# Index weights and index key in one unit of a two-block float32 transformer kernel, and VectorE's small jobs placed anew

## The reference

```python
cond = jax.nn.silu(c)
mod = (cond @ ada_w[l] + ada_b[l]).reshape(B, 6, D_MODEL)[:, :, None, :]
shift1, scale1, gate1 = mod[:, 0], mod[:, 1], mod[:, 2]
shift2, scale2, gate2 = mod[:, 3], mod[:, 4], mod[:, 5]
u = rmsnorm(x, norm_mix[l]) * (1.0 + scale1) + shift1
aq, ak, av, bq, bkv, biq, bik, biw, cq, ck, cv, g = split_cols(u @ w_in[l])
# index branch: 8 heads of 32, key bik (32 columns), head weights biw (8 columns)
s_idx = jax.nn.relu(jnp.einsum('bqhd,bkd->bqhk', iqb, ik))
score = jnp.einsum('bqhk,bqh->bqk', s_idx, iwb).astype(jnp.float32) * idx_scale
_, sel = lax.top_k(score, topk)          # topk = 64
# ... attention over the selected keys, two other attentions, gates, w_o
x = x + gate1 * (merged @ w_o[l])
u2 = rmsnorm(x, norm_mlp[l]) * (1.0 + scale2) + shift2
h = jnp.square(jax.nn.relu(u2 @ w_ff1[l]))
x = x + gate2 * (h @ w_ff2[l])
```

## Time and profile before

| | us |
|---|---|
| runs | 946.45, 946.54, 956.6; median 946.54 |
| profiled execution: its own time | 953.5 |
| its span, first to last instruction | 951.7 |
| TensorE busy in it | 923.2 (97%) |
| VectorE, ScalarE, GpSimd busy | 600.0, 498.3, 694.0 |
| mean granted TensorE clock | 0.985 of 2.4 GHz |

### The profile page before, as it was taken

How to read it: one execution, slowest core, us unless ns; L and a number is a source line. 1 busy time by engine, 2 the same in 40 slices (tenths; PEclk the granted TensorE clock), 3 DMA queues, 4 the chain that set the end, 5 groups by cost and what they waited for, 6 DMA issues and landing times.

```text
span 951.7 us, 21722 instructions
## 1 busy us (share of the span) xinstructions
PE 923.2 (97%) x7684; PEld 903.9 (95%) x7684; DVE 600.0 (63%) x1122; ACT 498.3 (52%) x820; POOL 694.0 (73%) x898
## 2 busy tenths in 40 slices
PE   5899999999999999999999999999999999999996
PEld 5898999989999999999999999999899999999996
DVE  3888878888785443532666677773346666877522
ACT  3555665574567664454644464444535444544451
POOL 1795669778778778877676679888827666788873
PEclk9999999999999999999999999999969999999999
DMA  9995448775545556555354546555514444455521
GB/s 359 415 359 192 165 178 292 289 260 183 178 158 198 205 187 249 194 204 177 136 178 174 176 136 219 177 184 198 194 45 170 149 168 150 160 211 187 201 87 45
DMA packets 28225, 185.22 MB, mean 195 GB/s; under 512 B 3027, under 2 KB 5504, under 8 KB 6272
## 3 DMA queue, kind: packets, MB, share of 16 engines
q1 hardware_dynamic: 25832, 167.93, 48.8%
q10 hardware_dynamic: 2328, 16.40, 4.7%
HBM read 183.26 MB, written 1.07 MB: 194 GB/s over the span
## 4 chain that ended last, share of the span: by engine, by line
PE 88%; DVE 6%; issue 2%; ACT 2%; DMA 1%; SPq 0%; POOL 0%; POOLq 0%; ACTq 0%; DVEq 0%
PE mm L609 26%; PE mm L611 25%; PE mm L610 25%; PE mm L643 1%; DVE score L1683 1%; PE mm L627 1%; PE mm L628 1%; PE mm L629 1%; ACT w_hi L1109 1%; PE ps_s L974 1%; PE ps_o L991 1%; PE ps_o L1065 1%; DMA hot<-onehot 1%; DVE ada_raw L1563 1%; DVE w_lo L1525 1%
## 5 line engine op out<-in xcount | busy, mean ns | idle before, releaser
L526 POOL TENSOR_TENSOR w_lo<-raw,w_hi 128x256 fp32r<-128x256 f32 x880 | 683.7, 814 | 235.2 <-ACT w_hi L1109 235.2
L609 PE MATMUL mm<-u_hi,w_hi 128*128 128x256 f32 x1568 | 447.8, 286 | 0.7 <-issue 0.6
L610 PE MATMUL mm<-u_lo,w_hi 128*128 128x256 f32 x1568 | 436.3, 278 | 0.0
L611 PE MATMUL mm<-u_hi,w_lo 128*128 128x256 f32 x1568 | 436.2, 278 | 0.0
L1109 ACT ACTIVATE w_hi<-raw 128x1024 fp32r<-128x1024 f32 x291 | 307.6, 1058 | 154.8 <-PE mm L611 148.5
L609 PEld LDWEIGHTS mm<-u_hi,w_hi 128*128 128x128 f32 x1568 | 296.4, 189 | 6.0 <-issue 5.3
L610 PEld LDWEIGHTS mm<-u_lo,w_hi 128*128 128x128 f32 x1568 | 296.4, 189 | 2.0 <-issue 1.9
L611 PEld LDWEIGHTS mm<-u_hi,w_lo 128*128 128x128 f32 x1568 | 296.6, 189 | 0.0
L1525 DVE TENSOR_TENSOR w_lo<-raw,w_hi 128x1024 fp32r<-128x1024 f32 x71 | 96.6, 1360 | 64.3 <-ACT w_hi L1109 55.2
L609 PE MATMUL mm<-h_hi,w_hi 128*128 128x256 f32 x256 | 70.8, 277 | 0.0
L610 PE MATMUL mm<-h_lo,w_hi 128*128 128x256 f32 x256 | 70.7, 276 | 0.0
(11 more groups left out here) (350 smaller groups left out, 1339.2 us busy)
## 6 DMA issues: line engine op xcount, KB each, us to landing
raw<-weights SPq DMA_DIRECT2D x145, 1024.0 KB, 4.8
ada_raw<-ada ACTq DMA_DIRECT2D x14, 1024.0 KB, 5.3
ada_raw<-ada SPq DMA_DIRECT2D x6, 1024.0 KB, 9.3
ada_more<-ada SPq DMA_DIRECT2D x4, 1024.0 KB, 12.1
bias<-tab_scratch SPq DMA_DIRECT2D x1, 1536.0 KB, 10.8
dec<-decay ACTq DMA_DIRECT2D x1, 1536.0 KB, 7.1
x<-xT SPq DMA_DIRECT2D x1, 1024.0 KB, 10.7
out<-x SPq DMA_DIRECT2D x4, 256.0 KB, 2.3
```

The lines of the kernel that those rows point to most:

```text
L526: ins = nc.gpsimd.tensor_tensor(lo[:, at], r[:, at], hi[:, at], ALU.subtract)
L609: nc.tensor.matmul(dst, wh, rhs_hi(k), start=a, stop=False)
L610: nc.tensor.matmul(dst, wh, rhs_lo(k), start=False, stop=False)
L611: i = nc.tensor.matmul(dst, wl, rhs_hi(k), start=False, stop=b)
```

## The change

One unit is taken out of the stream: the index key is now held three times in rows 0 to 95 of unit 0 and the 8 index weights in its rows 96 to 103. ACT takes the unit out of PSUM in three instructions (rows 0 to 95 of `ikT`, rows 96 to 127 of `ikT` from rows 0 to 31, and `iwf`). Everything behind unit 2 moves up by one number (290 units). So the tables of the attention are shifted by one, and the units whose `low` is VectorE's stand one place later in every stage. Besides, the index steps are regrouped, the selection rounds are placed anew, `ADA_AT` keeps 24 of 32 sums, and 8 sums (gate2, tiles 20 to 23) go behind eight units of the first MLP matrix, the last two tiles being loaded there from ACT's queue.

```diff
-N_QKV = 27
+N_QKV = 26
-C_IW, C_IQ, C_IK, C_KV, C_BQ = 0, 1, 3, 4, 5
-C_A = 9
-C_C = 21
+C_IW, C_IK, C_IQ, C_KV, C_BQ = 0, 0, 1, 3, 4
+C_A = 8
+C_C = 20
+IW_AT = 96
-    s_at = {12 + 3 * r: r for r in range(12)}
+    s_at = {11 + 3 * r: r for r in range(12)}
-    ADA_AT = [1, 2, 4, 7, 8, 10] + sorted([*range(16, 49, 3)] + [*range(26, 49, 3)] + [*range(30, 49, 3)])
-    LOAD_AT = {ADA_AT[2 * (n - 10) + 1] + 1: n for n in range(10, 24)}
-    IDX_AT = {6: [0], 7: [1], 8: [2, 3], 9: [4], 10: [5, 6], 11: [7]}
+    ADA_AT = [1, 2, 4] + sorted([*range(15, 48, 3)] + [*range(25, 48, 3)] + [44, 47])
+    LOAD_AT = {ADA_AT[2 * (n - 10) + 1] + 1: n for n in range(10, 22)}
+    ADA_F1 = {8: 0, 9: 1, 10: 2, 11: 3, 14: 4, 15: 5, 16: 6, 17: 7}
+    LOAD_F1 = {11: 22, 13: 23}
+    IDX_AT = {6: [0, 1], 7: [2], 8: [3, 4], 9: [5], 10: [6, 7]}
-    TOPK_AT = {10: [0] * 3, 11: [0] * 2, 12: [0], 13: [0] * 2, 16: [1] * 2, 18: [1] * 2, 19: [1], 21: [1] * 2, 22: [1]}
+    TOPK_AT = {10: [0] * 3, 11: [0], 12: [0] * 4, 14: [1], 15: [1] * 2, 17: [1], 18: [1] * 2, 20: [1], 21: [1]}
-    INV_AT = {27: 0, 33: 1, 36: 2, 39: 3}
-    ROOT_AT, FIN_AT, OAH_AT, OAL_AT = 41, 42, 44, 46
+    INV_AT = {26: 0, 32: 1, 35: 2, 38: 3}
+    ROOT_AT, FIN_AT, OAH_AT, OAL_AT = 40, 41, 43, 45
@@ qkv_evac, ScalarE
             if c == C_IW:
-                take_reversed(c, iwf[:, :], 8)
-            elif c < C_IK:
+                bank = bank_of(c)
+                A(ikT[0:IW_AT, :], bank[0:IW_AT, 0:T], ACT.Copy)
+                A(ikT[IW_AT:P, :], bank[0:P - IW_AT, 0:T], ACT.Copy)
+                A(iwf[:, :].rearrange("p (t q) -> p t q", t=QT),
+                  bank[IW_AT:IW_AT + 8, 0:T].rearrange("p (t q) -> p t q", t=QT)[:, :, ::-1], ACT.Copy)\
+                    .then_inc(taken[c % 4], 1)
+            elif c < C_KV:
                 take_reversed(c, iqT[:, c - C_IQ, :])
-            elif c == C_IK:
-                take(c, ikT[:, :])
@@ up_turn, ScalarE
+                if f in LOAD_F1:
+                    ada_load(act, LOAD_F1[f])
@@ VectorE, start of the first MLP matrix
                 low(None, U_F1 + SLOTS)
+                low(None, U_F1 + SLOTS + 1)
-        low(None, U_F1 + 2 * SLOTS)
+        for c in range(U_F1 + SLOTS + 2, U_F1 + 2 * SLOTS + 1):
+            low(None, c)
@@ up_turn, VectorE
+                if f in ADA_F1:
+                    ada_step(5 * KC + ADA_F1[f])
```

More of the change, by code:

```diff
@@ L390, in _build @@
     o_at = {c + 4: r for c, r in s_at.items()}
-    SUB_AT = {18 + 3 * h: h for h in range(NH)}
-    UV_AT = {29 + 3 * h: h for h in range(NH)}
-    VT_AT = {13 + 3 * h: 1 + h for h in range(NH)} | {25: 5, 28: 6}
-    ADA_AT = [1, 2, 4, 7, 8, 10] + sorted([*range(16, 49, 3)] + [*range(26, 49, 3)] + [*range(30, 49, 3)])
-    LOAD_AT = {ADA_AT[2 * (n - 10) + 1] + 1: n for n in range(10, 24)}
-    assert len(ADA_AT) == 4 * KC
-    IDX_AT = {6: [0], 7: [1], 8: [2, 3], 9: [4], 10: [5, 6], 11: [7]}
+    SUB_AT = {17 + 3 * h: h for h in range(NH)}
+    UV_AT = {28 + 3 * h: h for h in range(NH)}
+    VT_AT = {12 + 3 * h: 1 + h for h in range(NH)} | {24: 5, 27: 6}
+    ADA_AT = [1, 2, 4] + sorted([*range(15, 48, 3)] + [*range(25, 48, 3)] + [44, 47])
+    LOAD_AT = {ADA_AT[2 * (n - 10) + 1] + 1: n for n in range(10, 22)}
+    assert len(ADA_AT) == 3 * KC
+    ADA_F1 = {8: 0, 9: 1, 10: 2, 11: 3, 14: 4, 15: 5, 16: 6, 17: 7}
+    LOAD_F1 = {11: 22, 13: 23}
+    IDX_AT = {6: [0, 1], 7: [2], 8: [3, 4], 9: [5], 10: [6, 7]}
     HIGH_AT = {3: 8, 5: 9, 6: 10, 7: 11}
@@ L1818, in _ @@
                     .then_inc(S["oal_ready"], 1)
-        ada_read(dve, 6 * KC - 1)
+        ada_read(dve, 5 * KC - 1)
         o = O_BR
@@ L1949, in _ @@
         low(None, U_F2 - 1 + SLOTS)
+        ada_read(dve, 6 * KC - 1)
         V.tensor_tensor(nf_pre[:, :], vec[:, COLS["norm_final"]:COLS["norm_final"] + KC],
@@ L2241, in _stream @@
     aq, ak, av, bq, bkv, biq, bik, biw, cq, ck, cv, gate = [w_in[:, a:b] for a, b in zip(at[:-1], at[1:])]
-    parts = [_units(np.pad(biw, ((0, 0), (0, P - 8)))), _units(biq), _units(np.concatenate([bik] * 4, axis=1)),
+    parts = [_units(np.concatenate([bik] * 3 + [np.pad(biw, ((0, 0), (0, P - IW_AT - 8)))], axis=1)), _units(biq),
              _units(bkv), _units(bq)]
```

## The result

| | before | after |
|---|---|---|
| median, us | 946.61 | 954.24 |
| lowest to highest of 14 runs | 944.31 to 956.60 | 949.29 to 961.36 |
| profiled execution, span | 953.5, 951.7 | 961.36, 959.6 |

The ratio is 1.0072, 95% interval 1.0044 to 1.0100: the changed kernel is slower by 0.4 to 1.0%. Forecast were 944.0 us and a range of 938.0 to 951.0.

What follows compares the result with a forecast made beforehand. The prediction took TensorE's work plus the places where it stands still as the bound. Its terms summed to -2.5 us, taking the 946.5 median to 944.0, with an 8-in-10 range of 938.0 to 951.0.

Steps and rivals of the forecast that it cites:

- First MLP matrix: First MLP matrix: the wait for GpSimd's `w_lo` of the twelfth unit goes, -0.6 us; the eight sums there cost 0.
- One unit less: TensorE: 24 matmuls go with the removed unit, -2.9 us.
- rival 3: Until unit 22: VectorE sets the pace and its waits eat the removed unit's gain; 946.6 us, chance 0.2.
- Unit 0's way out of PSUM: Before unit 6: ScalarE does five copies instead of three before its bank may be written, +0.2 us.
- First: First `normalise`, transpose of head 0: TensorE waits 2.4 us instead of 1.8, +0.6.
- second normalise: Transpose of head 1: `low` and two rounds in block 15 make TensorE wait 2.1 us instead of 0.4, +1.7.
- Third normalise: Transpose of head 2: the low now stands behind `normalise`, so the 0.92 us wait ends, -0.9.
- Layers: Both layers: the first `low` now stands between q and k, so `kr` comes 0.35 and 0.55 us late, +0.9.
- last heads: Heads 9 and 10: the low now stands behind head 10's `normalise`, -0.8 us; head 9 counted 0.
- branches: Branch units: `low` goes one unit on, ending waits of 0.5 us at the second and 0.25 at the fifth, -0.75.
- 1 (the waits end): Heads 0 and 1: the waits for `normalise` go, and with the first the clock's fall; 938.3 us, chance 0.2.
- rival 2: Unit 17, behind the second `normalise`: the clock falls to half for long, costing 1.6 to 8.3 us; 952.3, chance 0.15.

Runs made afterwards that it cites:

- m1: Kernel before with only the unit merged; index steps, selection rounds and all 32 sums one block earlier: 946.72 us, ratio 1.0011.
- m2: Changed kernel with each of the eight sums in the first MLP matrix replaced by a copy of one column: 948.41 us, ratio 1.0020.
- b2: Changed kernel with the two selection rounds of block 15 put into block 14, nothing else: 951.55 us, ratio 1.0030.
- b3: Changed kernel with only the first half's selection rounds moved, from block 9 on: 955.59 us, ratio 1.0074.
- e7: Changed kernel with MLP sums three units apart, both halves' selection rounds moved, and a low in the layers put behind k's rotation: 942.05 us, ratio 0.9955.
- m3: Changed kernel with the condition row of the eight MLP sums copied once by VectorE to PSUM and read there: 950.96 us, ratio 1.0072.
- e8: Changed kernel with index steps and rounds of the kernel before, one block earlier, and the eight MLP sums three units apart: 945.05 us, ratio 0.9976.
- b1: Changed kernel with e7's selection rounds and the condition row of the dense MLP sums read from PSUM, copied by ScalarE: 941.54 us, ratio 0.9917.
- b4: Kernel before (291 units, nothing merged) with everything else of b1, its tables one block later: 947.39 us, ratio 0.9983.
- c1: b1 with ScalarE's row copy in halves behind units 8 and 9, and sums behind units 10 to 13 and 16 to 19: 941.06 us, ratio 0.9950.

## Why the prediction was wrong

**The step that failed** is *First MLP matrix*: "so it is behind by under 2 us with three banks free before TensorE minds: **0**". It asked who waits for VectorE and never which engine VectorE holds up while it works. The page had GpSimd busy for 694 us, and the trace of before showed the price in the same stage, by tile (least/median/longest ns of a quarter; the longest lie beside VectorE's lows):

```profile
L526 POOL TENSOR_TENSOR w_lo<-raw,w_hi x98: 720/742/1827, 267.2 to 358.1; 128x256 fp32r<-128x256 f32 x98
```

GpSimd has 1.9 us to spare in four units (four of 2.72, less twelve quarters of 0.75), of which a low takes up to 1.0; four sums in four units take 3.8 more. At the stop itself two sums and one low had run: three quarters at 1.7 instead of 0.74, 2.9 us more in a stretch of 5.8. Without the sums (m1, m2) TensorE waits 0.5, one unit later; with them 2.6. The stage was forecast at -0.6 and came out at +7.3. That is 7.9 of the 10.4 us between the forecast (-2.5) and the profiled difference (+7.9); the pace of 118 ns in `w_o` (0.8), the gates (0.9) and small terms make the rest. Of the 7.3, the sums are 5.6 to 6.0 (b2, b3) and the pace 1.0 to 1.3, which no step of mine could have had. The stage's -0.6 failed too: without any sums it takes 91.05 to 91.1 (m2, m1), 0.4 more than before, and that wait of 0.5 is still in it.

**What held.** *One unit less*, -2.9, is right as work, but m1 shows that by itself it bought nothing: rival 3 was right that the merge buys nothing, and in part for the reason it gave: of the 2.9 the projection kept 1.4, the waits at VectorE took the rest, and the gates (+1.5) the remainder. *Unit 0's way out of PSUM*, +0.2, is too small to be seen beside how much unit 6's start varies. *First* and *second normalise*: forecast waits 2.4 and 2.1, measured 2.84 and 2.37; of the walk of the blocks the rests at the ends of units 10 and 11 came (1.78 and 0.52, forecast 1.3 and 0.8), and a third of 2.25 at the end of unit 9, which the walk did not have. *Third normalise*: the wait is gone. *Layers*: +0.9 forecast, +1.3 measured. Mis-sized were *last heads* (-0.8, measured +0.1 for the gates: the wait of 0.8 is gone, but a wait of 0.5 for the last head's `prob` and one of 0.2 came, and of TensorE's 1.6 us of waits in the gates 1.1 are left) and *branches* (-0.75, measured -0.5, a wait of 0.6 for `merged` in its place).

**Rivals.** 1 (the waits end) did not happen, but its price, 5.7 us under the forecast, was about right: e7 ended them by moving four rounds, for 6.1 us. It was argued against with the very observation that held the remedy: the gaps lie before unit 11. 2 (a long fall of the clock behind the second normalise) didn't come in the profiled execution; m3 had a short one there (3.4 us, the lower end of its price) and 83.0 us for the projection. The long fall at the second layer is in five of the fifteen profiles read by stages, those of both kernels among them, and worth 6 to 8 us: second layer 257.8 to 259.3 with it, 251.05 to 251.5 without, which is about the distance between the two groups of times. That the median of before lies without it was assumed rightly, as far as mean clocks tell: about 0.994 in its runs near the median, 0.985 in the profiled one. The "under 1%" that rival 2 takes from the Trainium skill (TensorE: Matmul & The Clock Gate) is said there of the rise to full clock; the fall measured here, in mid-kernel, is 0.7 to 0.9% by itself.

## What to carry to other kernels

When work is moved on VectorE, price it on GpSimd too: here a VectorE instruction of 1024 float32 columns with both operands in SBUF took about a microsecond from GpSimd's subtraction, and that engine's slack, not VectorE's, said how densely such instructions may stand. One operand put in PSUM ended it, if the copy that puts it there isn't ahead of something that is waited for. And taking work away pays only where the rest is spread into the gaps it leaves: the merge with shifted tables bought nothing, and with three sums gone too and rounds put into the gaps the projection fell by 8.0 us.

## What the hardware showed unexpectedly

- TensorE at full granted clock ran at two paces, 113 and 118 ns between starts of the same matmuls, each kept for many units: 118 for units 86 to 97 and for `w_o` in the changed kernel (for `w_o` in e7 and e8 as well), for the last 20 units of MLP 1 in m3 and b1 and the last 21 in b4, for no such stretch in c1. That is up to 2.2 us in one stage. What sets it is open; it was not tried.
- The fall at the second layer kept the clock at half for 16.2 us and more although TensorE was busy all that time (before, 691.8 to 708.0: 16.20 us busy, 77 matmuls, clock 0.50).
- The releaser named for the longest new wait, ScalarE, had been done for nearly 4 us; the quarter of `w_lo` that came last was GpSimd's.
